# Softmax scale on ScalarE and the gate turned once per head pair, in an MLA and dilated-attention decoder trunk

## The chip, the cores and the metric

One core of one Trainium2 chip. The metric is the device time of one execution in microseconds (us); the kernel before was run three times.

## What is computed

The input is x, 256 tokens of width 2048, float32. Layer A is a multi-head latent attention layer of 16 heads, layer B a dilated sliding-window layer of 16 heads with three branches (dilations 1, 4, 16) that share one K/V. The change is in layer B. Cut to it:

```python
u = rms_norm(h, ln) @ w_in                     # queries of three branches, and a gate, per head
q = rms_norm(q_all[:, :, g], g_q[g])           # per branch g
s = where(valid, q @ k.T * E ** -0.5 + alibi, NEG_INF)
m = max(s); p = exp(s - m); den = sum(p)
o = p @ v / den                                # branches merged by their softmax denominators
return h + (o * silu(gate)) @ w_o
```

With 256 tokens the three branches are treated in one band of 384 scores for each head and each tile of 128 queries: 256 of branch 1 and 64 each of the residues of branches 4 and 16 on either half. One softmax over all of them gives the merged output.

## The kernel before

**Projections.** Every weight comes from HBM once, in steps of 128 x 1024 float32 (512 KB), through a ring of four slots (`RING`). SP issues the loads (L363). For each step ScalarE rounds the weights to float32r, the high part (`highs`, L478), VectorE subtracts to get the low part (`lows`, L794), and TensorE does three matmuls for each product (high by high, high by low, low by high; `three`, L1271): 12 matmuls of 512 columns per step. ScalarE may split a step once TensorE has used the slot three steps back (semaphore `slot_used`), VectorE follows ScalarE (`hi_ready`), and TensorE waits for VectorE (`lo_ready`).

**Layer B.** Its heads go in pairs, i = 0 to 7. A pair takes 40 steps, in 20 quarters s = 0 to 19 of two steps (`b_pair`, on every engine). Five accumulators follow each other: queries of branches 1 and 4 (Q01), keys of the same (K01), key of 16 and value of 1 (K2V0), values (V12), query of 16 and gate (Q2GATE). VectorE scales the rows by their reciprocal root mean square (`b_rows`, L864) and turns them in blocks of 32 (`b_blocks`, L1180), and ScalarE applies the gains (`gain_of`, L766). The gate's SiLU is computed by ScalarE and VectorE in `gate_tanhs` and `gates` at s = 19 and lies in `gate[:, 0]`, tokens on partitions.

**Attention** of pair i - 1 runs beside the projection of pair i, for i = 1 to 7, and the last beside the output projection (i = `PAIRS`), there at the steps `B_LAST_SLOTS` of one step each. A pair has four units u (two heads, two query tiles). `b_units(s)` gives the stages of a quarter: stage 0 of unit u is at s = u + 2, stage 1 one quarter later, and so on:

- stage 0: TensorE scores (`b_score`, L1514, L1519), VectorE adds the bias and takes the maximum (`band_mask`, L886, L891), ScalarE takes the exponential with its sum (`unit_exp`, L532)
- stage 1: VectorE takes the reciprocal of the sum (`unit_den`, L915) and multiplies the gate by it into `og` (`band_gate`, L899); both stand in `b_gates`, at the head of a quarter, in front of its first low part. TensorE turns three blocks of probabilities and `og` in one bank (`band_turn`, L1303), and ScalarE copies all 512 columns to `probT` (`unit_turned`, L516)
- stage 2: TensorE multiplies by the values (`band_pv`, L1536, L1540), VectorE multiplies by the turned gate (`band_out`, L904)
- stage 3: ScalarE and VectorE split the output in high and low (`band_store`, `band_low`).

In its order of work an engine does, in quarter s: TensorE the 24 projection matmuls and then its stages; ScalarE the first split, its stages (3, then 1, then 0), the second split; VectorE `b_gates`, the first low part, its stages 3, 2, 0, sums and blocks, the second low part. The query blocks of Q2GATE for the attention of pair i - 1 come at s = 0 and s = 1 of pair i, eight in each:

```python
if s < 2:
    for n in range(8 * s, 8 * s + 8):
        last = b_blocks(Q2GATE, 3, n)
    if s == 1:
        last.then_inc(blocked, 1)
```

`b_score` of unit 0 waits for ScalarE's gain of this query (`gained`), which waits for `blocked`. The order of every engine is written out by hand; all engines but TensorE run the middle pairs (2 to 7 in layer B, two per turn) in a hardware loop (`Fori`), TensorE has them written out.

## Time and profile before

| | |
|---|---|
| median of 3 runs | 1404.21 us (1403.74 to 1404.41) |
| the profiled execution's own time | 1404.01 us |
| its span | 1402.2 us |
| TensorE, VectorE, ScalarE, GpSimd busy | 99%, 75%, 50%, 7% of the span |
| TensorE's share of the chain that ended last | 94% |
| DMA | 252.49 MB, mean 180 GB/s |

The profile is of one execution. Its busy times are per engine; a TensorE matmul is pipelined, so its duration is longer than the distance to the next one, and start-to-start distances tell more. The time of the execution is its span and 1.8 us around it.

### The profile page before, as it was taken

The numbers are of one execution on the slowest core, as the hardware profiler recorded it, in microseconds if no ns is written. First come the engines' busy times: TensorE is split into PE (matmuls) and PEld (weight loads), VectorE is DVE, ScalarE is ACT, GpSimd is POOL, SyncE is SP. The second block draws the span as 40 slices with busy tenths as digits, with TensorE's granted clock in tenths as the row PEclk, the third lists the DMA queues.
The fourth block names the chain that finished last, engine by engine and source line by source line (L and its number), as shares of the span: only waits on it lengthen the run. The fifth ranks groups of instructions, "written<-read, shape, count | busy, mean of one in ns | idle before, by whom it ended". The sixth has DMA issues, their size and how long they took to land.

```text
span 1402.2 us, 20187 instructions
## 1 busy us (share of the span) xinstructions
PE 1395.2 (99%) x6648; PEld 1169.4 (83%) x6648; DVE 1046.5 (75%) x1969; ACT 706.6 (50%) x1032; POOL 102.5 (7%) x67
## 2 busy tenths in 40 slices
PE   9999999999999999999999999999999999999999
PEld 6888888888888888888888888888888888888887
DVE  6767767747667868877877877887887788789653
ACT  6555555646544544544544454544454445454442
POOL 0101001000010001000101100101010110010000
PEclk9999999999999999999999999999999999999999
DMA  9653544455556545645654654565556456555544
GB/s 355 232 173 125 166 143 142 147 190 179 183 187 203 191 151 180 205 155 180 182 194 149 197 181 163 183 198 167 166 188 189 159 186 194 160 181 190 171 165 150
DMA packets 71233, 252.49 MB, mean 180 GB/s; under 512 B 7904, under 2 KB 8288, under 8 KB 71136
## 3 DMA queue, kind: packets, MB, share of 16 engines
q1 hardware_dynamic: 70704, 249.95, 54.7%
q10 hardware_dynamic: 432, 1.31, 0.3%
q8 instruction: 53, 0.87, 0.2%
q14 instruction: 44, 0.36, 0.1%
HBM read 249.14 MB, written 2.10 MB: 179 GB/s over the span
## 4 chain that ended last, share of the span: by engine, by line
PE 94%; DVE 2%; issue 2%; ACT 1%; DMA 0%; POOL 0%; SPq 0%; DVEq 0%; POOLq 0%
PE acc L1271 85%; PE turn L1303 1%; PE score L1514 1%; PE pv_bank L1536 1%; PE score L1519 1%; PE pv_bank L1540 1%; DVE qT L1180 1%; PE pv_bank L1315 1%; PE score L1411 1%; PE score L1413 1%; DVE w_lo L794 1%; PE turn L1397 0%; DMA raw<-in_w_in 0%; PE og_bank L1323 0%; POOL rms L426 0%
## 5 line engine op out<-in xcount | busy, mean ns | idle before, releaser
L794 DVE TENSOR_TENSOR w_lo<-raw,w_hi 128x1024 fp32r<-128x1024 f32 x463 | 574.2, 1251 | 205.9 <-ACT w_hi L478 196.9
L478 ACT ACTIVATE w_hi<-raw 128x1024 fp32r<-128x1024 f32 x463 | 482.4, 1050 | 397.2 <-PE acc L1271 386.0
L1271 PE MATMUL acc<-w_hi,xa_hi 128*128 128x512 f32 x956 | 378.7, 396 | 0.6 <-DVE w_lo L794 0.4
L1271 PE MATMUL acc<-w_hi,xa_lo 128*128 128x512 f32 x956 | 372.8, 390 | 0.0
L1271 PE MATMUL acc<-w_lo,xa_hi 128*128 128x512 f32 x956 | 372.2, 389 | 0.0
L1271 PE MATMUL acc<-w_hi,xb_hi 128*128 128x512 f32 (+1 forms) x640 | 249.4, 390 | 0.0
L1271 PE MATMUL acc<-w_hi,xb_lo 128*128 128x512 f32 (+1 forms) x640 | 245.9, 384 | 0.0
L1271 PE MATMUL acc<-w_lo,xb_hi 128*128 128x512 f32 (+1 forms) x640 | 245.5, 384 | 0.0
L1271 PEld LDWEIGHTS acc<-w_hi,xa_lo 128*128 128x128 f32 x956 | 179.4, 188 | 37.9
L1271 PEld LDWEIGHTS acc<-w_hi,xa_hi 128*128 128x128 f32 x956 | 179.6, 188 | 37.5 <-issue 1.3
L1271 PEld LDWEIGHTS acc<-w_lo,xa_hi 128*128 128x128 f32 x956 | 179.7, 188 | 35.3
L426 POOL TENSOR_TENSOR rms<-ms,mhalf 128x4 f32<-128x4 f32 (+2 forms) x50 | 73.2, 1465 | 1050.6 <-DVE ms L850 855.4
L1271 PEld LDWEIGHTS acc<-w_hi,xb_lo 128*128 128x128 f32 x640 | 120.1, 188 | 22.7
L1271 PEld LDWEIGHTS acc<-w_lo,xb_hi 128*128 128x128 f32 x640 | 120.3, 188 | 22.1
L1271 PEld LDWEIGHTS acc<-w_hi,xb_hi 128*128 128x128 f32 x640 | 120.2, 188 | 22.0
L1180 DVE STREAM_TRANSPOSE kT<-rows 32x128 f32<-32x128 f32 x384 | 102.2, 288 | 4.5
L1271 PE MATMUL acc<-w_hi,oT_hi 128*128 128x512 f32 x256 | 102.3, 400 | 0.0
L1271 PE MATMUL acc<-w_hi,oT_lo 128*128 128x512 f32 x256 | 100.0, 391 | 0.0
L1271 PE MATMUL acc<-w_lo,oT_hi 128*128 128x512 f32 x256 | 99.7, 390 | 0.0
L1180 DVE STREAM_TRANSPOSE qT<-rows 32x256 f32<-32x256 f32 (+1 forms) x256 | 94.5, 369 | 4.1
L532 ACT ACTIVATE prob<-prob,top_neg 128x128 f32<-128x128 f32 (+1 forms) x64 | 34.3, 537 | 91.3 <-DVE top_neg L891 63.9
L516 ACT ACTIVATE probT<-turn 128x128 f32<-128x128 f32 (+1 forms) x64 | 29.7, 463 | 76.7 <-PE turn L1303 57.2
(178 smaller groups left out, 1061.4 us busy)
## 6 DMA issues: line engine op xcount, KB each, us to landing
raw<-in_w_b SPq DMA_DIRECT2D x320, 512.0 KB, 3.6
raw<-in_w_out_a SPq DMA_DIRECT2D x32, 512.0 KB, 3.3
raw<-in_w_out_b SPq DMA_DIRECT2D x32, 512.0 KB, 3.3
raw<-in_w_gate SPq DMA_DIRECT2D x30, 512.0 KB, 3.6
raw<-in_w_kv SPq DMA_DIRECT2D x16, 512.0 KB, 4.3
raw<-in_w_in SPq DMA_DIRECT2D x15, 512.0 KB, 6.2
raw<-in_w_q SPq DMA_DIRECT2D x16, 384.0 KB, 3.0
res<-in_x_tok SPq DMA_DIRECT2D x4, 512.0 KB, 7.8
```

What stands on the lines that cost most here:

```text
L426: nc.gpsimd.tensor_tensor(rms[:, 0:width], ms[:, 0:width], mhalf[:, 0:width], ALU.pow)\
L478: nc.scalar.activation(w[0][:, s, 0:width], raw[:, s, 0:width], ACT.Copy).then_inc(hi_ready, 1)
L516: last = nc.scalar.activation(dst, turn[:, 0:width], ACT.Copy)
L532: nc.scalar.activation(prob[:, u % 2, 0:width], prob[:, u % 2, 0:width], ACT.Exp, bias=top_neg[:, u:u + 1], accum_out=den[:, u:u + 1])\
L794: nc.vector.tensor_tensor(w[1][:, s, 0:width], raw[:, s, 0:width], w[0][:, s, 0:width].bitcast(F32), ALU.subtract).then_inc(lo_ready, 1)
L1180: last = nc.vector.transpose(dst, src)
L1271: last = nc.tensor.matmul(out, x(a), y(b), start=start and k == 0, stop=stop and k == 2, **more)
L1303: last = nc.tensor.transpose(turn[:, col:col + P], src, ident[:])
L1315: last = nc.tensor.matmul(pv, probT[:, k * P:(k + 1) * P], val, start=k == 0, stop=k == len(values) - 1)
L1411: nc.tensor.matmul(score[:, 0:n], qT[:, par * 512 + at:par * 512 + at + P], kT[:, k_0 + h * SEQ:k_0 + h * SEQ + n], start=True, stop=False)
L1413: nc.tensor.matmul(score[:, 0:n], q_ropes[par][:, at:at + P], kT[:, k_0 + 512:k_0 + 512 + n], start=False, stop=True).then_inc(scored, 1)
L1514: nc.tensor.matmul(score[:, P:P + SEQ], qT[:, h * SEQ + t * P:h * SEQ + (t + 1) * P], kT[:, h * SEQ:(h + 1) * SEQ], start=True, stop=True)
```

## The change

- `band_gate` is gone. In its place ScalarE multiplies the probabilities of a unit by the reciprocal sum in place, in stage 1, after a wait for `den_ready`, and TensorE's turn waits for that (`prob_scaled`). ScalarE's wait for `out_made` ahead of its copy is gone, and the copy has 384 columns.
- TensorE turns three blocks per unit instead of four. VectorE turns the gates of a pair, in 16 blocks of 32x128 from `gate[:, 0]` to `gate[:, 1]` (`gate_turn`): eight at s = 1 and eight at s = 2, there ahead of the mask of unit 0. `band_out` reads them there.
- All 16 query blocks of Q2GATE stand at s = 0.
- K01's blocks of both groups are one transpose of 32x256 each instead of two of 32x128.
- All `Fori` loops, on SP, GpSimd, ScalarE and VectorE, are Python loops: the instructions are written out. The diff shows two of them.

```diff
--- before.py
+++ after.py
@@ -216,6 +216,7 @@
         og_bank = ctx.enter_context(nc.psum_tensor("og_bank", [P, 512], F32))
         pv = pv_bank[:, 0:P]
         ogT = og_bank[:, 0:P]
+        gate_T = gate[:, 1].rearrange("p t d -> p (t d)")
         h_banks = (pv_bank, og_bank, score)
 
         def cst(name):
@@ -331,6 +332,8 @@
         den_ready = sem("den_ready")
         pv_ready = sem("pv_ready")
         og_ready = sem("og_ready")
+        prob_scaled = sem("prob_scaled")
+        gate_turned = sem("gate_turned")
         og_turned = sem("og_turned")
         o_ready = sem("o_ready")
         out_made = sem("out_made")
@@ -389,16 +392,16 @@
                     else:
                         load((i, MLA_STEPS), MLA_0 + s, w_gate[i, s - 2 if s < 4 else s - 4], STEP)
 
-            with sp.Fori(0, PAIRS - 1) as i:
+            for i in range(0, PAIRS - 1):
                 mla_pair(i, MLA_STEPS)
             mla_pair(PAIRS - 1, LAST_STEPS)
...
@@ -708,9 +711,10 @@
                     if stage == 3:
                         band_store((i - 1) * UNITS + u, i - 1, u)
                     if stage == 1:
-                        if u:
-                            act.wait_ge(out_made, (i - 1) * UNITS + u)
-                        unit_turned(b_round(i, u), u, BAND + P)
+                        act.wait_ge(den_ready, U + 1)
+                        at = prob[:, u % 2, 0:BAND]
+                        nc.scalar.activation(at, at, ACT.Copy, scale=den_inv[:, u:u + 1]).then_inc(prob_scaled, 1)
+                        unit_turned(b_round(i, u), u, BAND)
                     if stage == 0:
                         unit_exp(U, u, BAND)
 
@@ -891,17 +895,24 @@
                 nc.vector.tensor_scalar(top_neg[:, u:u + 1], top[:, u:u + 1], -1.0, None, ALU.mult)\
                     .then_inc(top_ready, 1)
 
-            def band_gate(U, u, g, gates_so_far):
+            def gate_turn(i, part):
+
+                if part == 0:
+                    dve.wait_ge(gate_done, i + GATE_FILLS)
+                for n in range(8 * part, 8 * part + 8):
+                    a, b = n // 4, n % 4
+                    src = gate[a * QUAD:(a + 1) * QUAD, 0].rearrange("p t (u d) -> p t u d", d=P)
+                    dst = gate_T[b * QUAD:(b + 1) * QUAD].rearrange("p (u t d) -> p t u d", t=TILES, d=P)
+                    last = nc.vector.transpose(dst[:, :, :, a * QUAD:(a + 1) * QUAD], src[:, :, :, b * QUAD:(b + 1) * QUAD])
+                if part == 1:
+                    last.then_inc(gate_turned, 1)
+
+            def band_out(U, i, u):
 
                 if u == 0:
-                    dve.wait_ge(gate_done, gates_so_far)
-                dve.wait_ge(den_ready, U + 1)
-                nc.vector.tensor_scalar(og[:, u % 2], g, den_inv[:, u:u + 1], None, ALU.mult).then_inc(og_ready, 1)
-
-            def band_out(U, u):
-
+                    dve.wait_ge(gate_turned, i)
                 dve.wait_ge(pv_ready, U + 1)
-                nc.vector.tensor_tensor(out[:, u % 2], pv, probT[:, BAND:BAND + P], ALU.mult).then_inc(out_made, 1)
+                nc.vector.tensor_tensor(out[:, u % 2], pv, gate_T[:, u * P:(u + 1) * P], ALU.mult).then_inc(out_made, 1)
 
             def band_low(U, i, u):
 
@@ -1163,38 +1174,39 @@
                     if stage == 1:
                         U = (i - 1) * UNITS + (B_UNIT_0 + u)
                         unit_den(U, u)
-                        band_gate(U, u, gate[:, 0, u % 2, (u // 2) * P:(u // 2 + 1) * P], i + GATE_FILLS)
 
             def b_blocks(f, k, n):
 
                 buf, x = (B_CHAIN_0 + k) % 2, qT if f in (Q01, Q2GATE) else kT
                 a, b = n // 4, n % 4
-                for first, groups, swap in {Q01: [(0, 2, 0)], K01: [(0, 1, 0), (1, 1, 1)], K2V0: [(0, 1, 1)],
-                                            Q2GATE: [(0, 1, 0)]}[f]:
-                    at = (first + 2 * (f in (K2V0, Q2GATE))) * 2 * SEQ
-                    col = QUAD * (a ^ 2 if swap else a)
-                    src = rows[a * QUAD:(a + 1) * QUAD, buf, :, first * 2 * P:(first + groups) * 2 * P]\
-                        .rearrange("p t (u d) -> p t u d", d=P)[:, :, :, b * QUAD:(b + 1) * QUAD]
-                    dst = x[b * QUAD:(b + 1) * QUAD, at:at + groups * 2 * SEQ]\
-                        .rearrange("p (u t d) -> p t u d", t=TILES, d=P)[:, :, :, col:col + QUAD]
-                    last = nc.vector.transpose(dst, src)
-                return last
+                groups = 2 if f in (Q01, K01) else 1
+                at, swapped = (0, 1) if groups == 2 else (2, 2)
+                if f in (Q01, Q2GATE):
+                    swapped = GROUPS
+                cols = [(at + g) * 2 * SEQ + QUAD * (a ^ 2 if at + g >= swapped else a) for g in range(groups)]
+                src = rows[a * QUAD:(a + 1) * QUAD, buf, :, 0:groups * 2 * P]\
+                    .rearrange("p t (g u d) -> p t g u d", u=2, d=P)[:, :, :, :, b * QUAD:(b + 1) * QUAD]
+                to = x[b * QUAD:(b + 1) * QUAD, cols[0]:cols[0] + QUAD]
+                parts = [list(d) for d in to.ap]
+                dst = bass.AP(to.tensor, to.offset, [parts[0], [P, TILES], [cols[-1] - cols[0] or QUAD, groups],
+                                                    [SEQ, 2], [1, QUAD]])
+                return nc.vector.transpose(dst, src)
 
             def b_attend(i, s, par_before):
                 if s == 0:
                     b_rows(i - 1, par_before, 3)
                     dve.wait_ge(rows_ready, i * 4 + B_CHAIN_0)
-                if s < 2:
-                    for n in range(8 * s, 8 * s + 8):
+                    for n in range(16):
                         last = b_blocks(Q2GATE, 3, n)
-                    if s == 1:
-                        last.then_inc(blocked, 1)
+                    last.then_inc(blocked, 1)
+                if s in (1, 2):
+                    gate_turn(i, s - 1)
                 for stage, u in b_units(s):
                     U = (i - 1) * UNITS + (B_UNIT_0 + u)
                     if stage == 3:
                         band_low(U, i - 1, u)
                     if stage == 2:
-                        band_out(U, u)
+                        band_out(U, i, u)
                     if stage == 0:
                         band_mask(U, (i - 1) * UNITS + u, u, alibi[:, u // 2, u % 2], i - 1)
 
@@ -1244,7 +1256,7 @@
 
             b_pair(0, 0, False)
             b_pair(1, 1, True)
-            with dve.Fori(0, (PAIRS - 2) // 2) as t:
+            for t in range(0, (PAIRS - 2) // 2):
                 b_pair(t * 2 + 2, 0, True)
                 b_pair(t * 2 + 3, 1, True)
             for k in range(OUT_STEPS):
@@ -1521,10 +1533,8 @@
 
             def band_turn(U, u, rnd):
 
-                pe.wait_ge(prob_ready, U + 1)
-                pe.wait_ge(og_ready, U + 1)
-                turn_rows(rnd, [(prob[:, u % 2, k * P:(k + 1) * P], k * P) for k in range(BAND // P)]
-                          + [(og[:, u % 2], BAND)])
+                pe.wait_ge(prob_scaled, U - B_UNIT_0 + 1)
+                turn_rows(rnd, [(prob[:, u % 2, k * P:(k + 1) * P], k * P) for k in range(BAND // P)])
 
             def band_pv(U, B, u, rnd):
```

How this moves the instructions, at three places. VectorE, from the gate's last operation at s = 19 to the first unit's reciprocal, beside pair 1 (`w_lo` is the low part of a step, `qT` the query blocks, `prob` the mask). Before:

```order
L935 TENSOR_SCALAR gate<-gate,r_half 128x256 x2
L794 TENSOR_TENSOR w_lo<-raw,w_hi 128x1024 x2
L864 TENSOR_TENSOR rows<-acc,rms 128x2x256
L1180 STREAM_TRANSPOSE qT<-rows 32x2x2x32 x8
L794 TENSOR_TENSOR w_lo<-raw,w_hi 128x1024 x2
L1180 STREAM_TRANSPOSE qT<-rows 32x2x2x32 x8
L794 TENSOR_TENSOR w_lo<-raw,w_hi 128x1024 x2
L886 ISA prob,top<-score,phase 64x384
```

After:

```order
L946 TENSOR_SCALAR gate<-gate,r_half 128x256 x2
L798 TENSOR_TENSOR w_lo<-raw,w_hi 128x1024 x2
L868 TENSOR_TENSOR rows<-acc,rms 128x2x256
L1193 STREAM_TRANSPOSE qT<-rows 32x2x2x32 x16
L798 TENSOR_TENSOR w_lo<-raw,w_hi 128x1024 x2
L906 STREAM_TRANSPOSE gate<-gate 32x2x2x32 x8
L798 TENSOR_TENSOR w_lo<-raw,w_hi 128x1024 x2
L906 STREAM_TRANSPOSE gate<-gate 32x2x2x32 x8
L890 ISA prob,top<-score,phase 64x384
```

The gate's 16 blocks stand between the rows and the first mask, as do all query blocks, before and now. ScalarE, beside pair 1, from the query's gain on (`w_hi` is the high part of a step, `rows<-acc` the squares). After:

```order
L770 ACTIVATE qT<-qT,gain 128x512
L535 ACTIVATE prob,den<-prob,top_neg 128x384
L481 ACTIVATE w_hi<-raw 128x1024 x2
L716 ACTIVATE prob<-prob,den_inv 128x384
L519 ACTIVATE probT<-turn 128x384
L535 ACTIVATE prob,den<-prob,top_neg 128x384
L512 ACTIVATE rows<-acc 128x1024
L481 ACTIVATE w_hi<-raw 128x1024 x2
L716 ACTIVATE prob<-prob,den_inv 128x384
```

The scale by the reciprocal sum (L716) is new; it stands behind the two splits and in front of the copy of the turned bank. VectorE in the last pair, now:

```order
L868 TENSOR_TENSOR rows<-acc,rms 128x2x256
L1193 STREAM_TRANSPOSE qT<-rows 32x2x2x32 x16
L798 TENSOR_TENSOR w_lo<-raw,w_hi 128x1024
L906 STREAM_TRANSPOSE gate<-gate 32x2x2x32 x8
L798 TENSOR_TENSOR w_lo<-raw,w_hi 128x1024 x2
L906 STREAM_TRANSPOSE gate<-gate 32x2x2x32 x8
L890 ISA prob,top<-score,phase 64x384
```

Before, eight query blocks, one low part, eight query blocks and two low parts stood between those rows and the mask.

## Rows read from the trace of the kernel before

**Rows 1.** Page, busy us (share of the span) and instructions.

```profile
PE 1395.2 (99%) x6648; PEld 1169.4 (83%) x6648; DVE 1046.5 (75%) x1969; ACT 706.6 (50%) x1032; POOL 102.5 (7%) x67
```

**Rows 2.** Groups by form: line, engine, op, names, shapes, xcount | busy us, mean ns | idle before.

```profile
L1180 DVE STREAM_TRANSPOSE kT<-rows 32x128 f32<-32x128 f32 x384 | 102.2, 288 | 4.5
...
L1180 DVE STREAM_TRANSPOSE qT<-rows 32x256 f32<-32x256 f32 x128 | 55.7, 435 | 2.1
...
L532 ACT ACTIVATE prob<-prob,top_neg 128x384 f32<-128x384 f32 x32 | 19.8, 617 | 63.9 <-DVE top_neg L891 63.9
...
L766 ACT ACTIVATE qT<-qT,gain 128x512 f32<-128x512 f32 x24 | 16.3, 709 | 4.0 <-DVE qT L1180 4.0
```

**Rows 3.** Timeline of PE, beside the projection of pair 2: start us, us, what, xcount.

```profile
609.89 0.60 PE L1514 MATMUL score<-kT,qT 128*128 128x256 f32 x2
610.32 0.61 PE L1519 MATMUL score<-kT,qT 128*128 128x128 f32 x4
610.68 0.48 PE L1271 MATMUL acc<-w_hi,xb_hi 128*128 128x512 f32 x1
...
616.23 0.49 PE L1303 MATMUL turn<-ident,prob 128*128 128x128 f32 x3
616.56 0.27 PE L1303 MATMUL turn<-ident,og 128*128 128x128 f32 x1
616.67 0.60 PE L1514 MATMUL score<-kT,qT 128*128 128x256 f32 x2
...
624.00 0.52 PE L1303 MATMUL turn<-ident,prob 128*128 128x128 f32 x3
```

**Rows 4.** Timeline of DVE, the same stretch; [idle us <-releaser].

```profile
594.39 0.69 DVE L845 TENSOR_REDUCE ss<-rows 128x4 f32<-128x512 f32 x1 [1.03 <-ACT rows L509]
...
599.55 2.51 DVE L1180 STREAM_TRANSPOSE qT<-rows 32x128 f32<-32x128 f32 x8
602.08 2.36 DVE L794 TENSOR_TENSOR w_lo<-raw,w_hi 128x1024 fp32r<-128x1024 f32 x2
...
607.03 1.23 DVE L794 TENSOR_TENSOR w_lo<-raw,w_hi 128x1024 fp32r<-128x1024 f32 x1
608.46 1.23 DVE L794 TENSOR_TENSOR w_lo<-raw,w_hi 128x1024 fp32r<-128x1024 f32 x1 [0.20 <-ACT w_hi L478]
611.16 0.55 DVE L886 CUSTOM_DVE_ANT_0 prob<-score,phase 64x384 f32<-64x384 f32 x1 [1.48 <-PE score L1519]
...
615.36 0.15 DVE L915 RECIPROCAL den_inv<-den 128x1 f32<-128x1 f32 x1
615.62 0.29 DVE L899 TENSOR_SCALAR og<-gate,den_inv 128x128 f32<-128x128 f32 x1
```

**Rows 5.** Timeline of ACT, behind unit 0's mask.

```profile
613.14 1.99 ACT L478 ACTIVATE w_hi<-raw 128x1024 fp32r<-128x1024 f32 x2
```

**Rows 6.** Timeline of DVE, unit 1 of the same pair.

```profile
623.61 0.29 DVE L899 TENSOR_SCALAR og<-gate,den_inv 128x128 f32<-128x128 f32 x1
```

**Rows 7.** Timeline of DVE and PE at the turn of the loop.

```profile
835.88 1.23 DVE L794 TENSOR_TENSOR w_lo<-raw,w_hi 128x1024 fp32r<-128x1024 f32 x1 [2.41 <-issue]
...
845.35 0.39 PE L1271 MATMUL acc<-w_hi,xb_lo 128*128 128x512 f32 x1
845.99 0.70 PE L1514 MATMUL score<-kT,qT 128*128 128x256 f32 x2 [0.25 <-ACT qT L766]
```

**Rows 8.** Timeline of DVE, last pair.

```profile
1306.59 2.51 DVE L1180 STREAM_TRANSPOSE qT<-rows 32x128 f32<-32x128 f32 x8
...
1315.21 0.54 DVE L886 CUSTOM_DVE_ANT_0 prob<-score,phase 64x384 f32<-64x384 f32 x1
```

**Rows 9.** Timeline of PE, last pair.

```profile
1313.71 0.70 PE L1514 MATMUL score<-kT,qT 128*128 128x256 f32 x2 [0.93 <-ACT qT L766]
...
1320.17 0.49 PE L1303 MATMUL turn<-ident,prob 128*128 128x128 f32 x3
```

**Rows 10.** Timeline of PE at the start; then windows: us, busy (x), PEclk, DMA.

```profile
1.85 4.99 PE L1340 MATMUL score<-probT 128*128 128x512 f32 x6 [1.85 <-POOL v L416]
...
1399.00:1402.20 3.20, 0.07 (x1) 0.00 (x0) 0.69 (x1) 0.00 (x0) 0.00 (x0) 1.00 0.44 164
1402.20:1404.00 1.80, 0.00 (x0) 0.00 (x0) 0.00 (x0) 0.00 (x0) 0.00 (x0) 0.51 0.00 0
```

More of the change, by code:

```diff
@@ L390, in mla_pair @@
                         load((i, MLA_STEPS), MLA_0 + s, w_gate[i, s - 2 if s < 4 else s - 4], STEP)
-            with sp.Fori(0, PAIRS - 1) as i:
+            for i in range(0, PAIRS - 1):
                 mla_pair(i, MLA_STEPS)
             mla_pair(PAIRS - 1, LAST_STEPS)
-            with sp.Fori(0, OUT_STEPS // 8) as j:
+            for j in range(0, OUT_STEPS // 8):
                 for q in range(8):
                     load((j, 8), OUT_A_0 + q, w_out_a[j, q], STEP)
-            with sp.Fori(0, PAIRS) as i:
+            for i in range(0, PAIRS):
                 for s in range(B_STEPS):
                     load((i, B_STEPS), B_0 + s, w_b[i, s], STEP)
-            with sp.Fori(0, OUT_STEPS // 8) as j:
+            for j in range(0, OUT_STEPS // 8):
                 for q in range(8):
@@ L432, in _ @@
             chain(1, TILES)
-            with pool.Fori(0, PAIRS) as i:
+            for i in range(0, PAIRS):
                 for s in range(MLA_STEPS):
@@ L459, in _ @@
             b_pair(0, False)
-            with pool.Fori(1, PAIRS) as i:
+            for i in range(1, PAIRS):
                 b_pair(i, True)
@@ L672, in _ @@
             mla_pair(1, 1, 1)
-            with act.Fori(0, (PAIRS - 4) // 2) as t:
+            for t in range(0, (PAIRS - 4) // 2):
                 mla_pair(t * 2 + 2, 0, 2)
@@ L777, in _ @@
             b_pair(1, 1, True)
-            with act.Fori(0, (PAIRS - 2) // 2) as t:
+            for t in range(0, (PAIRS - 2) // 2):
                 b_pair(t * 2 + 2, 0, True)
@@ L1126, in _ @@
             mla_pair(1, 1, 1, 0)
-            with dve.Fori(0, (PAIRS - 4) // 2) as t:
+            for t in range(0, (PAIRS - 4) // 2):
                 mla_pair(t * 2 + 2, 0, 2, t + 1)
@@ L1246, in _ @@
             b_pair(1, 1, True)
-            with dve.Fori(0, (PAIRS - 2) // 2) as t:
+            for t in range(0, (PAIRS - 2) // 2):
                 b_pair(t * 2 + 2, 0, True)
```

## The prediction

> **What bounds the kernel now.** I read the page's busy times first: TensorE (PE) is busy for 99% of the span [rows 1]. So the time is the sum of TensorE's own work and its waits, and an edit counts only through these two. Then I read the first units beside the projection of pair 2 of layer B in the timeline, one engine at a time. On TensorE two score groups and one turn group show the rhythm of a unit: score, 24 projection matmuls, turn, score [rows 3]. On VectorE the reader is to see which stretches have no idle time in front, and where it does wait [rows 4]. ScalarE's row there gives the two operations that sit between the exponential and the next split [rows 5].
>
> The link that matters is the one behind the first mask of a pair. The mask of unit 0 starts at 611.16, the reciprocal of the denominator ends at 615.51, the scaled gate at 615.91, and TensorE turns at 616.23 [rows 3, 4]. Between mask and reciprocal lie the exponential, two splits on ScalarE, of which VectorE's next low part needs the first, and that low part itself [rows 4, 5]: 4.35 us from mask to reciprocal. So before the change the turn has 0.3 us to spare, and VectorE as a whole has 0.20 us and 1.48 us of idle time ahead of the mask, 1.68 us together [rows 4]. That is the whole reserve of this stretch. It can't be enlarged by work saved earlier in the pair, since VectorE waits at 594.39 for the squares that end the projection of the pair before [rows 4], and everything from there to 608.26 runs without a gap.
>
> **The change, part by part.**
>
> (a) *TensorE's turn of the gate goes.* One 128x128 turn takes 0.11 us from start to start (616.56 to 616.67) [rows 3]. 32 units: -3.5 us, all of it on the path.
>
> (b) *VectorE turns the gates, in 16 pieces of 32x128 per pair.* The nearest row is the query blocks of the same shape: 8 in 2.51 us, 0.314 each [rows 4]. Per pair 5.03 us. Eight come in step 1 and eight in step 2, both ahead of the first mask; the 16 query blocks, now all in step 0, were ahead of it before too. So 5.03 us of new work meets 1.68 us of reserve, and the mask starts 3.35 us later, at 614.5.
>
> (c) *ScalarE scales the probabilities, VectorE no longer scales the gate.* The scale is 128x384 in SBUF. The nearest rows are the exponential on the same tile, 617 ns, and the 128x512 gain in place, 709 ns [rows 2]; I take 0.60. It replaces 0.29 on VectorE [rows 4] in the same place of the chain. For unit 0: 615.51 + 3.35 + 0.05 to hand over + 0.60 + 0.10 = 619.6, where TensorE was ready at 616.23: **3.4 us of new wait per pair**. Seven pairs run this way beside projections: +23.7.
>
> (d) *Unit 1.* Its turn already waited: the scaled gate ends at 623.90, the turn starts at 624.00 [rows 3, 6]. The chain is the same, with 0.60 in the place of 0.29 and a shorter turn of unit 0, whose gain stands in (a): +0.33, seven times +2.3. Units 2 and 3 have 0.8 us more room, since no squares of a chain lie in their link: 0.
>
> (e) *The written-out loops.* At the loop's turn VectorE stood 2.41 us for issue, and the first score of that pair started 0.64 us after the last projection matmul, where such matmuls begin 0.23 apart (24 of them from 610.68 to 616.23), and then took 0.1 us longer [rows 3, 7]: 0.5 us, at two turns of this loop, -1.0. Elsewhere the loops' register instructions cost nothing that I find: from mask to turn it is 5.07 us in a loop pair and 4.96 in the last pair, which was never in a loop [rows 3, 4, 8, 9], and that 0.1 is TensorE's, not the chain's.
>
> (f) *The last pair* runs beside the output projection, in steps half as long. VectorE has no gap from 1306.59 to the mask at 1315.21 [rows 8]. Now 16 query blocks (5.03), one low part (1.23), 8 gate pieces (2.52), two low parts (2.36) and 8 gate pieces (2.52) come first: mask at 1320.3. The turn follows 4.35 + 0.75 = 5.1 us later, at 1325.4, against 1320.17 [rows 9]: +5.3. The query blocks are ready earlier, so the 1.1 us that TensorE lost ahead of its score at 1313.71 goes, but that is inside the 5.3, as it only lengthens the later wait.
>
> (g) *Both K groups in one transpose.* 128 of 32x256 at 435 ns take the place of 256 at 288 [rows 2]: VectorE saves 18 us over the kernel, in steps 10 to 17. It lies ahead of the wait at 594.39, so nothing of it reaches TensorE: 0. ScalarE's copy of the turned bank is 128 columns shorter and no longer waits for VectorE's output product; the exponential behind it waits for the mask anyway: 0.
>
> Sum: -3.5 + 23.7 + 2.3 - 1.0 + 5.3 = **+26.8**, on the profiled execution's 1404.0: 1430.8.
>
> (h) *TensorE's clock.* In the trace it is granted in full (2.4 GHz) as long as TensorE works; 3.1 us after the last matmul it falls to the lower level, 1.2 GHz [rows 10]. At the start, six 128x512 float32 matmuls took 4.99 us, about 0.8 us from start to start, where 256 columns take 0.22 [rows 3, 10]: the lower level, for some 4.5 us, which costs 2.2 us. In the last pair TensorE will be ready at about 1319.5 (its score 1.1 us earlier than before, a low part behind the gate pieces 0.4 us later) and stand until 1325.4, for 5.9 us, so I count one fall there; the seven waits of 3.4 us are barely longer than the 3.1 us in the row, and I count one or two falls among them at a little under 2.2 each. That makes +3.7 and the forecast **1434.5**. The profiled execution lies 0.2 us below the median of 1404.21, which changes nothing.
>
> A rule of the Trainium skill, "TensorE: Matmul & The Clock Gate", section on HAM oscillation, says that a TensorE that idles between groups of matmuls is throttled to half and starts the next group cold, each time. By that rule the sum would be that of rival 1. "VectorE: DVE Perf Modes", rules for kernel authors, speaks against the change: a 128x128 transpose belongs on TensorE if PSUM will do. Here 32 turns of 0.11 us on TensorE become 128 pieces of 0.314 on VectorE, and the trace bears the rule out as far as VectorE's reserve is gone; with a reserve of 5 us the rule would be wrong here by the 3.5 us of (a).
>
> **Rivals.**
>
> 1. *Every wait lets the clock fall.* Then eight falls of 2.2: 1430.8 + 17.6 = 1448.4. For it: the fall at 3.1 us. Against it: seven waits are hardly longer, and the few small matmuls around them are work too. Chance 0.13.
>
> 2. *The waits are smaller than I think.* The gate pieces run as fast as the K blocks, whose mean is 288 ns where the query blocks begin 314 ns apart [rows 2, 4], so at 0.28 at best, and the scale takes 0.45. That is 0.5 and 0.15 less per pair, 5.2 in eight, and the clock doesn't fall: 1430.8 - 5.2 = 1425.6. For it: the shapes are alike. Against it: the gate's pieces are written with the query blocks' pattern. Chance 0.12.
>
> 3. *VectorE's reserve covers the gate pieces (the other side).* If VectorE's order left the first mask at its old place, only (a), (d), (e) and the vanished 1.1 us would be left: 1404.0 - 3.5 + 2.3 - 1.0 - 1.1 = 1400.7, or 0.24% faster. It decides at 1.7 to 2.0 us of work ahead of the mask: the pieces would have to take 0.12 us each, or most of them to run behind the mask. The order of the program and the row at 2.51 us speak against it. Chance 0.06.
>
> 4. *The program doesn't do what it says.* VectorE's longer stream of written-out instructions could also stall for fetching, as at the loop's turn, or the five-dimensional transposes of K could run piece by piece and be no faster than two; both make VectorE later, but before the wait at 594.39 there is slack. Within 5 us of the forecast, either way. Chance 0.05, inside the range.
>
> **Numbers.** Forecast 0.64, the rivals 0.13, 0.12, 0.06, 0.05. The range reaches down past rival 2, by the 0.4 us that each of eight waits may be off, and up to rival 1: 1422 to 1448. A difference of 0.2% (2.8 us) is about what can be told from none. Slower by more than that: all but rival 3 and what lies between it and rival 2, 0.91; within it 0.03; faster 0.06, rival 3.
>
> **What would show it.** In the profile of the changed kernel, TensorE's turn of unit 0 should wait for ScalarE's scaling by about 3.4 us in seven pairs and by about 6 in the last; between the query blocks and the first mask VectorE should have no idle time; the turn of unit 1 should wait some 0.5 us; the score's wait for the query gain should be gone. The granted clock should show a dip near 1325. I am wrong if the first mask starts less than 1 us behind its score, if the gate pieces take under 0.2 us, or if TensorE's waits are at a projection, for a low part, and not at the turn.

## The result, and the profile after

The changed kernel takes 1437.44 us, the median of four runs (1435.33 to 1438.38), where the kernel before takes 1404.2. The ratio is 1.0236, with a 95% interval of 1.0224 to 1.0248: 2.4% slower, 3 us above the forecast. The profiled execution took 1438.38 us, with a span of 1436.4 us against 1402.2 before: 34.2 us to account for.

The page of the kernel after, busy us by engine and then the chain that ended last:

```profile
PE 1403.3 (98%) x6616; PEld 1173.8 (82%) x6616; DVE 1065.1 (74%) x1937; ACT 723.2 (50%) x1064; POOL 101.5 (7%) x67
...
PE 84%; DVE 13%; ACT 2%; issue 1%; DMA 0%; POOL 0%; SPq 0%; ACTq 0%; DVEq 0%
```

TensorE has 32 matmuls fewer than before [rows 1] and is busy for longer: part of its work ran at a lower clock, as the windows below show. Its share of the chain fell from 94% to 84%, and VectorE stands in the chain with 13%. The page's 40 slices are no help here; the waits are only a few microseconds each.

The groups by form (line, engine, operation, names, shapes, count, busy us, mean ns, idle before) that answer to [rows 2], and the new ones:

```profile
L1193 DVE STREAM_TRANSPOSE kT<-rows 32x256 f32<-32x256 f32 x128 | 55.8, 436 | 2.6
...
L906 DVE STREAM_TRANSPOSE gate<-gate 32x128 f32<-32x128 f32 x128 | 38.7, 303 | 1.8
...
L716 ACT ACTIVATE prob<-prob,den_inv 128x384 f32<-128x384 f32 x32 | 19.7, 616 | 11.3 <-DVE den_inv L926 11.3
...
L1315 PE MATMUL turn<-ident,prob 128*128 128x128 f32 x144 | 27.6, 284 | 27.4 <-ACT prob L716 27.4
```

The last row names the loss: TensorE stood 27.4 us in front of its turns, waiting for ScalarE's scaled probabilities. The gate pieces and the scale cost what they were taken for, 303 and 616 ns.

Where that wait comes from stands in the timeline beside the projection of pair 2, the stretch of [rows 3]. TensorE (start us, us, what, count, idle before and its releaser), and then score, last matmul and turn of unit 0 in the last pair:

```profile
614.86 0.60 PE L1526 MATMUL score<-kT,qT 128*128 128x256 f32 x2
...
620.97 0.39 PE L1283 MATMUL acc<-w_hi,xb_lo 128*128 128x512 f32 x1
624.39 0.55 PE L1315 MATMUL turn<-ident,prob 128*128 128x128 f32 x3 [3.03 <-ACT prob L716]
...
632.36 0.55 PE L1315 MATMUL turn<-ident,prob 128*128 128x128 f32 x3 [0.21 <-ACT prob L716]
...
1340.00 0.59 PE L1526 MATMUL score<-kT,qT 128*128 128x256 f32 x2
...
1346.61 0.39 PE L1283 MATMUL acc<-w_hi,oT_lo 128*128 128x512 f32 x1
1352.70 0.90 PE L1315 MATMUL turn<-ident,prob 128*128 128x128 f32 x3 [5.70 <-ACT prob L716]
```

Matmuls of 512 columns begin 0.23 us apart, so TensorE was ready at 621.20 and stood 3.19 us; in the last pair it was ready at 1346.84 and stood 5.86. (The brackets say a little less, because the end of a matmul is modelled. Starts are what I count with.)

VectorE in the same stretch, the rows that answer to [rows 4], with ScalarE's scale behind the reciprocal, and then the last pair's mask:

```profile
599.36 0.69 DVE L849 TENSOR_REDUCE ss<-rows 128x4 f32<-128x512 f32 x1 [1.03 <-ACT rows L512]
...
604.52 5.05 DVE L1193 STREAM_TRANSPOSE qT<-rows 32x128 f32<-32x128 f32 x16
609.60 2.36 DVE L798 TENSOR_TENSOR w_lo<-raw,w_hi 128x1024 fp32r<-128x1024 f32 x2
611.88 2.50 DVE L906 STREAM_TRANSPOSE gate<-gate 32x128 f32<-32x128 f32 x8
614.39 2.36 DVE L798 TENSOR_TENSOR w_lo<-raw,w_hi 128x1024 fp32r<-128x1024 f32 x2
616.78 2.52 DVE L906 STREAM_TRANSPOSE gate<-gate 32x128 f32<-32x128 f32 x8
619.34 0.55 DVE L890 CUSTOM_DVE_ANT_0 prob<-score,phase 64x384 f32<-64x384 f32 x1
...
623.53 0.16 DVE L926 RECIPROCAL den_inv<-den 128x1 f32<-128x1 f32 x1
623.72 0.61 ACT L716 ACTIVATE prob<-prob,den_inv 128x384 f32<-128x384 f32 x1 [0.42 <-DVE den_inv L926]
...
1347.65 0.55 DVE L890 CUSTOM_DVE_ANT_0 prob<-score,phase 64x384 f32<-64x384 f32 x1
```

Behind the read of the squares at 599.36 there is no bracket on any row up to the mask: VectorE never waits. The two idle pieces of [rows 4], 0.20 and 1.48 us, are gone, and the mask comes 19.98 us after that read where it came 16.77 after it before. It starts 4.5 us behind the start of its score. From there the chain is as long as it was: mask to turn 5.05 us (5.07 before), because the 0.6 of the scale replaced the 0.29 of the gate's product and the 0.3 us that the turn had to spare.

The second loss stands in the granted clock. Windows of 12 us around four of the first-unit waits (window, length, busy us and counts of PE, PEld, DVE, ACT, POOL, then PEclk, DMA share, GB/s):

```profile
497.00:509.00 12.00, 8.95 (x31) 7.13 (x30) 6.10 (x14) 7.20 (x11) 0.69 (x1) 0.72 0.30 90
620.00:632.00 12.00, 8.97 (x48) 7.36 (x46) 7.28 (x16) 7.54 (x12) 1.48 (x1) 1.00 0.30 97
742.00:754.00 12.00, 8.95 (x38) 7.25 (x37) 7.05 (x13) 7.52 (x12) 1.89 (x1) 0.86 0.27 87
...
1346.00:1358.00 12.00, 6.30 (x23) 5.06 (x22) 6.53 (x19) 4.84 (x9) 0.00 (x0) 0.72 0.47 146
```

Of the seven waits beside projections, all of 3.19 to 3.21 us, three more have 0.86 and one more has 1.00: the clock fell at five of seven and in the last pair. What a fall does to the work shows in TensorE's rows behind the first of these waits:

```profile
497.56 0.39 PE L1283 MATMUL acc<-w_hi,xb_lo 128*128 128x512 f32 x1
501.00 0.90 PE L1315 MATMUL turn<-ident,prob 128*128 128x128 f32 x3 [3.05 <-ACT prob L716]
...
505.54 0.63 PE L1283 MATMUL acc<-w_hi,xa_lo 128*128 128x512 f32 x1
505.96 0.63 PE L1283 MATMUL acc<-w_hi,xa_hi 128*128 128x512 f32 x1
...
507.41 0.39 PE L1283 MATMUL acc<-w_lo,xa_hi 128*128 128x512 f32 x1
507.64 0.40 PE L1283 MATMUL acc<-w_hi,xa_lo 128*128 128x512 f32 x1
...
511.45 0.50 PE L1315 MATMUL turn<-ident,prob 128*128 128x128 f32 x3
```

At the lower level (1.2 GHz) matmuls begin 0.42 us apart, then 0.23 again. From the turn of unit 0 to that of unit 1 it takes 10.45 us here and 7.97 in pair 2 (624.39 to 632.36), where the clock did not fall.

### The profile page after: what moved, and what is told of

Same layout as the page of the kernel before. It is cut to its first block, busy times and chain, and to the rows that moved or that the text cites. A ratio compares the mean times of both kernels' runs of the same rounds, so it can differ in the third digit from the quotient of the medians.

```text
span 1436.4 us, 17781 instructions
## 1 busy us (share of the span) xinstructions
PE 1403.3 (98%) x6616; PEld 1173.8 (82%) x6616; DVE 1065.1 (74%) x1937; ACT 723.2 (50%) x1064; POOL 101.5 (7%) x67
## 4 chain that ended last, share of the span: by engine, by line
PE 84%; DVE 13%; ACT 2%; issue 1%; DMA 0%; POOL 0%; SPq 0%; ACTq 0%; DVEq 0%
PE acc L1283 75%; DVE w_lo L798 5%; DVE qT L1193 3%; DVE gate L906 3%; PE turn L1315 1%; PE pv_bank L1546 1%; PE score L1531 1%; PE pv_bank L1550 1%; PE score L1526 1%; DVE prob L890 1%; PE pv_bank L1327 1%; PE score L1423 1%; PE score L1425 1%; DVE ss L849 1%; ACT rows L512 1%
## 5 line engine op out<-in xcount | busy, mean ns | idle before, releaser
L1193 DVE STREAM_TRANSPOSE kT<-rows 32x256 f32<-32x256 f32 (+1 forms) x256 | 94.5, 369 | 4.5
L512 ACT ACTIVATE rows<-acc 128x512 f32<-128x512 f32 (+2 forms) x50 | 39.0, 780 | 38.8 <-PE acc L1283 38.8
```

The costliest lines, as they stand in the source:

```text
L512: nc.scalar.activation(rows[:, buf, :, 0:width], acc[:, pair, :, 0:width], ACT.Square)\
L1193: return nc.vector.transpose(dst, src)
```

## The experiments

Two theories were to be told apart. **Order**: the time comes from the gate pieces standing ahead of the first mask, with VectorE's reserve exceeded, and the clock adds to it. **Parts**: the new operations cost it, the scale on ScalarE above all, or the written-out loops. Each kernel below was timed against the kernel before on its own chip (medians 1403.82 to 1404.01).

### Leaving the gate's transposes out: e1_no_gate_turn

```diff
-                if u == 0:
-                    dve.wait_ge(gate_turned, i)
...
-                if s in (1, 2):
-                    gate_turn(i, s - 1)
```

> The change without VectorE's turn of the gates (its 16 transposes per pair and the wait for them are left out, so layer B's output is multiplied by what lies in the second half of the gate tile instead of the gate). Theory: the 5.03 us of transposes ahead of the first mask are the cause of the waits of 3.2 us (seven) and 5.9 us (one) and, through them, of the clock's falls. Then all of these go: unit 0's turn waits at most 0.3 us, and the time is 1404.2 - 3.5 (TensorE's turns) - 1.0 (loops) - 1.1 (score of the last pair) + 1.5 (unit 1) = about 1400. Rival: ScalarE's scale in the link, or all 16 query blocks in one quarter, is what makes unit 0 late: then waits of 1 us or more stay at unit 0 and the time stays above 1410.

Measured: 1402.28 us, ratio 0.9988 (0.9979 to 0.9997). The waits of its TensorE (line, releaser, total us, times, longest):

```profile
PE turn L1311 <- ACT prob L716: 2.9, 8, 1.0
```

The whole rest of the change, scale included, is a gain of 1.7 us. All seven waits of unit 0 beside projections are gone, the clock never fell, and what is left is 0.4 us at unit 1 (0.7 in one pair) and 1.2 at unit 0 of the last pair. That last wait was not expected. It is the 1.1 us of the score's wait, moved to the turn: in that pair VectorE had no gap before the change either [rows 8], and from the last turn of the pair before to this one it takes 90.40 us, against 90.56 before the change. So the transposes on VectorE carry 35.2 us, though VectorE is idle for a quarter of the span.

### The loops alone: e2_loops_only

```diff
-            with dve.Fori(0, (PAIRS - 2) // 2) as t:
+            for t in range(0, (PAIRS - 2) // 2):
```

The same edit at every `Fori` of the kernel before.

> The kernel before with all hardware loops written out and nothing else. Theory: only the stall of the score at two turns of layer B's loop goes, 0.5 us each: 1403.2, that is 1.0 us faster. Rival: the register instructions on VectorE and ScalarE or the loops of layer A cost more than I find: 1400 or less. Second rival: the longer program costs fetching: 1405 or more.

Measured: 1402.63 us, ratio 0.9990 (0.9981 to 0.9999), 1.4 us less; the forecast had 1.0. The two late scores behind the loop's turn are gone; the score of the last pair still waits:

```profile
PE score L1514 <- ACT qT L766: 0.9, 1, 0.9
```

### The same waits with TensorE kept at work: e3_busy_wait

```diff
+                if u == 0:
+                    for _ in range(24 if rnd == b_round(PAIRS, 0) else 12):
+                        nc.tensor.matmul(og_bank[:], xa[0][:, 0, 0:P], ..., start=True, stop=True)
                 pe.wait_ge(prob_scaled, U - B_UNIT_0 + 1)
```

> The change with TensorE kept at work during its wait for unit 0: 12 matmuls of 512 columns into a bank that nothing reads, ahead of the wait (24 in the last pair), 2.7 us of the 3.2 and 5.4 of the 5.9. Theory: the clock no longer falls, and the 11.5 us that its low stretches cost in the trace go, the waits stay: about 1426, granted clock 1.00 throughout. Rival: the low stretches cost nothing of their own, since VectorE's chain would hold TensorE anyway: 1437 or more.

Measured: 1429.94 us, ratio 1.0183 (1.0168 to 1.0199). Its TensorE at the same place:

```profile
619.65 2.88 PE L1538 MATMUL og_bank<-xa_hi 128*128 128x512 f32 x12
622.86 0.55 PE L1315 MATMUL turn<-ident,prob 128*128 128x128 f32 x3 [0.33 <-ACT prob L716]
```

The turn comes no earlier: 3.21 us behind the moment TensorE was ready, against 3.19. But the granted clock is 1.00 throughout. With the waits' length kept, the falls are worth 1437.44 - 1429.94 = 7.5 us by the medians, 8.2 by the two spans. The spans also differ by something that isn't the clock: this trace has a wait in its very first steps that the changed kernel's hasn't.

```profile
13.41 0.48 PE L1283 MATMUL acc<-w_hi,xa_hi 128*128 128x512 f32 x1 [0.58 <-DVE w_lo L798]
```

Behind it TensorE runs 0.9 us later, and its first turn still does (501.87 against 501.00); the kernel before has such a wait too, of 0.41 us, at 13.04. Without it the falls are worth 9.1 by the spans. I had expected 1426, taking the whole loss in the slow stretches for the price. It isn't: behind a fall the second turn has no wait left (511.45 above stands without a bracket), while here it waits 0.4 us in every pair. A fall costs 9.2 - 8.0 = 1.2 us in four pairs (745.37 to 754.58 is 9.21), 2.5 in the first, where the slow stretch is twice as long, and 2.0 in the last.

### Six of sixteen pieces moved behind the second mask: e4_moved

```diff
-                if s in (1, 2):
-                    gate_turn(i, s - 1)
+                if s == 1 and i < PAIRS:
+                    gate_turn(i, 0, 5)
+                if s == 4 and i == PAIRS:
+                    gate_turn(i, 10, 16)
...
+                        if u < 2:
+                            gate_turn(i, *(((0, 5), (5, 10)) if i == PAIRS else ((5, 10), (10, 16)))[u])
```

`gate_turn` takes first and last piece here. Five pieces stand ahead of the first mask, five behind it, six behind the second.

> The change with the 16 gate transposes of a pair in other places: 5 ahead of the first mask (1.57 us, inside the reserve of 1.68), 5 behind the first mask and 6 behind the second, where VectorE waits for ScalarE's exponential and split anyway; in the last pair 5, 5 and 6 behind the masks of units 0 and 1 and ahead of unit 0's output. Theory: it is only where the transposes stand that costs; the mask starts as before, unit 0's turn waits 0.3 to 0.5 us, no fall of the clock: 1401 to 1404, at or below the time of before. Rival: VectorE's work as such is too much in these quarters, and the transposes behind the masks make units 1 or 2 late instead: 1410 or more.

Measured: 1403.85 us, ratio 0.9999 (0.9990 to 1.0008). VectorE's first mask, and TensorE's two turns, beside pair 2:

```profile
607.15 1.55 DVE L906 STREAM_TRANSPOSE gate<-gate 32x128 f32<-32x128 f32 x5
608.72 2.36 DVE L798 TENSOR_TENSOR w_lo<-raw,w_hi 128x1024 fp32r<-128x1024 f32 x2
611.40 0.55 DVE L890 CUSTOM_DVE_ANT_0 prob<-score,phase 64x384 f32<-64x384 f32 x1 [0.32 <-PE score L1535]
...
616.48 0.53 PE L1319 MATMUL turn<-ident,prob 128*128 128x128 f32 x3
...
624.69 0.55 PE L1319 MATMUL turn<-ident,prob 128*128 128x128 f32 x3 [0.49 <-ACT prob L716]
```

Every instruction of the change is still there, and 33.6 us are gone. The mask waits for its score again. Five pieces take 1.55 us and 0.32 are left, so the reserve is 1.87 us, a little more than the 1.68 that the brackets of [rows 4] add up to. **Order** it is. Unit 1 pays a little, 0.67 us a pair (8.21 from turn to turn, where e5_early_den below has 7.54 without a wait), since six pieces now stand ahead of its reciprocal.

### The reciprocal right behind the mask: e5_early_den

```diff
                         if u < 2:
                             gate_turn(...)
+                        unit_den(U, u)
...
-                    if attend:
-                        b_gates(i, s)
                     lows((i, B_STEPS), B_0 + 4 + 2 * s)
```

On top of e4_moved, and the same in the last pair.

> As the run with the moved gate transposes (1403.85), and the reciprocal of a unit's sum stands right behind its mask on VectorE instead of behind the low part that follows. Theory: what is left as waits there, 0.65 us at unit 1 in seven pairs and 1.2 us at unit 0 of the last, comes from the reciprocal's place behind the squares' sums and the low part; ScalarE's scale then follows its second split at once, 5.5 us behind the mask at unit 1 where TensorE comes 5.9 behind it. The seven waits go (-4.6) and 0.4 of the last: 1399 us, 0.35% faster than before. Rival: ScalarE itself is late, or VectorE's wait for the exponential now holds up the sums and low parts: 1402 or more.

Measured: 1398.37 us against 1403.83, ratio **0.9960 (0.9947 to 0.9974)**: 0.4% faster than the kernel before, a small gain but clear of the noise. Unit 1's reciprocal (VectorE), its scale (ScalarE) and the turns (TensorE):

```profile
618.69 1.90 DVE L906 STREAM_TRANSPOSE gate<-gate 32x128 f32<-32x128 f32 x6
620.62 0.16 DVE L926 RECIPROCAL den_inv<-den 128x1 f32<-128x1 f32 x1
...
622.12 0.60 ACT L716 ACTIVATE prob<-prob,den_inv 128x384 f32<-128x384 f32 x1
...
615.78 0.49 PE L1309 MATMUL turn<-ident,prob 128*128 128x128 f32 x3
...
623.31 0.50 PE L1309 MATMUL turn<-ident,prob 128*128 128x128 f32 x3
```

In e4_moved this reciprocal ran at 623.84, behind a low part; here it is done before ScalarE's split ends, the scale follows without a bracket, and both turns stand directly behind their matmuls. One wait is left in layer B, 0.64 us in the last pair.

### The early reciprocal without the swap: e8_early_gate

On e2_loops_only, `unit_den` and `band_gate` moved behind `band_mask` in the same way, and nothing else of the change.

> The kernel before with its loops written out (1402.63) and the reciprocal and the scaled gate right behind the mask, TensorE's turn of the gate kept. It tells what of a gain of the early reciprocal needs the change at all. Theory: unit 1's wait of 0.12 us in seven pairs goes, nothing else: 1401.8; the 3.5 us of TensorE's 32 turns are then the difference to the version with the early reciprocal on the changed kernel, less the last pair's wait. Rival: the early reciprocal alone does as much, 1399 or less, and the change brings nothing.

Measured: 1401.5 us, ratio 0.9984 (0.9975 to 0.9993). This is 2.3 us less than the kernel before. So of e5's 5.5 us, 1.4 are the loops, 1.0 the earlier reciprocal (turn to turn 7.62 us in place of 7.74), and 3.1 the rest of the change. That rest is the swap for the most part: a pair lasts 117.31 us in e5_early_den and 117.70 here, 0.39 for four turns that were priced at 0.11 each. It also has the moved query blocks, the K transposes and the last pair's waits (0.64 us at the turn there, 1.1 at the score here), which no run takes apart.

### The scale's price: e7_scale_twice

```diff
-                        ... scale=den_inv[:, u:u + 1]).then_inc(prob_scaled, 1)
+                        ... scale=den_inv[:, u:u + 1]).then_inc(scaled_once, 1)
+                        act.wait_ge(scaled_once, (i - 1) * UNITS + u + 1)
+                        nc.scalar.activation(at, at, ACT.Copy, scale=1.0).then_inc(prob_scaled, 1)
```

On e4_moved: a second pass over the probabilities.

> As the run with the moved gate transposes (1403.85), and ScalarE passes over the probabilities a second time with factor 1.0, 0.6 us more in the link from reciprocal to turn. Theory: the scale stands wholly in the link: unit 1's wait grows from 0.65 to 1.3, unit 0's from 0 to about 0.4 and the last pair's by 0.65: 7 x 1.05 + 0.65 = 8.0, 1411.9. Rival: ScalarE has time there and the scale is hidden: 1405 or less.

Measured: 1411.97 us, ratio 1.0058 (1.0043 to 1.0073), 8.1 us above e4_moved.

```profile
PE turn L1322 <- ACT prob L719: 11.5, 15, 1.6
```

All of the second pass lands on the path of units 0 and 1, none of it on units 2 and 3: 0.53 at unit 0 and 0.59 at unit 1 in seven pairs, 0.56 in the last, 8.4 in all. The scale is on the path; it is cheap because 0.6 replaced 0.29 and 0.3 of slack.

### The query blocks back in two eights: e6_blocks_8_8

```diff
-                    for n in range(16):
-                        last = b_blocks(Q2GATE, 3, n)
-                    last.then_inc(blocked, 1)
+                if s < 2:
+                    for n in range(8 * s, 8 * s + 8):
+                        last = b_blocks(Q2GATE, 3, n)
+                    if s == 1:
+                        last.then_inc(blocked, 1)
```

> The change with the query blocks at their old places, eight in each of the first two quarters. Theory: what counts is the sum of VectorE's work ahead of the first mask, which stays: 1436 to 1438, the seven waits still 3.2 us. Rival: all 16 in one quarter hold up the low parts and so the splits: 1434 or less.

Measured: 1439.21 us, ratio 1.0250 (1.0234 to 1.0266), 1.8 above the changed kernel and 1.2 above the range expected. The seven waits are 3.32 us, the clock fell at six of them, and the last pair's score waits again:

```profile
1342.54 0.70 PE L1528 MATMUL score<-kT,qT 128*128 128x256 f32 x2 [0.93 <-ACT qT L770]
```

So that move of the change takes away the score's wait, which lies inside the later one, as (f) said: the turn waits 5.28 us here and 5.86 there, and from the last turn of the pair before to this one it takes 95.73 and 95.59 us. It takes 0.1 us off each of the seven. Two medians of four runs, 1.8 us apart with a different number of falls, say little beyond that.

### Twelve and fourteen pieces ahead: e9_ahead_12, e10_ahead_14

```diff
-                    gate_turn(i, s - 1)
+                    gate_turn(i, *((0, 8), (8, 12))[s - 1])
...
+                        if u == 0:
+                            gate_turn(i, 12, 16)
```

With 14 in place of 12 in the second. They set the length of the wait, to see how the clock's falls go with it.

> The change with 12 of the 16 gate transposes ahead of the first mask and 4 behind it. It asks whether the falls of the clock hang on the length of the wait. Theory: the waits shrink by 4 x 0.314 = 1.25 us, from 3.2 to 1.9 in seven pairs and from 5.9 to 4.6 in the last; the clock no longer falls in the seven, where it fell five times of seven at 3.2, and may fall once in the last. With 10.0 less of waits and some 5 less of low clock: 1421 to 1424. Rival: the falls hang on the number of waits and not on their length; they stay, and the time is 1427 or more.

> The change with 14 of the 16 gate transposes ahead of the first mask and 2 behind it. Theory: waits of 2.6 us in seven pairs and 5.2 in the last, 5.0 less in sum; the clock falls at fewer of the seven than at 3.2 us, none to two of them: 1425 to 1431. Rival: as often as at 3.2 us: 1432 or more.

Measured: 1422.31 us, ratio 1.0132 (1.0115 to 1.0149), and 1429.77 us, ratio 1.0186 (1.0169 to 1.0203). The seven waits are 1.9 and 2.5 us. A piece moved ahead makes the wait 0.31 us longer. Windows of e9_ahead_12 around the second wait and of the last pair:

```profile
616.00:628.00 12.00, 10.02 (x53) 8.17 (x52) 8.53 (x18) 7.84 (x12) 2.05 (x1) 1.00 0.38 118
...
1330.00:1342.00 12.00, 7.59 (x31) 6.07 (x30) 7.56 (x20) 5.86 (x10) 0.00 (x0) 0.86 0.48 162
```

e10_ahead_14, the second and third waits, in windows and in TensorE's timeline:

```profile
617.50:629.50 12.00, 9.61 (x50) 7.84 (x49) 7.88 (x20) 7.26 (x12) 1.20 (x1) 1.00 0.39 124
739.00:751.00 12.00, 9.62 (x40) 7.66 (x39) 7.79 (x15) 7.74 (x12) 2.23 (x1) 0.86 0.33 96
...
622.17 0.55 PE L1317 MATMUL turn<-ident,prob 128*128 128x128 f32 x3 [2.39 <-ACT prob L716]
742.48 0.55 PE L1317 MATMUL turn<-ident,prob 128*128 128x128 f32 x3 [2.38 <-ACT prob L716]
```

The two waits are the same to 0.01 us, and the clock fell at one of them; in all it fell at three of the seven, where at most two were expected. Over the four kernels, with the falls of the profiled execution of each and the mean granted clock of all four runs of each:

| wait of unit 0 | kernel | clock fell | mean clock, four runs |
|---|---|---|---|
| 1.9 us | e9_ahead_12 | 0 of 7 | 0.998 to 0.999 |
| 2.5 us | e10_ahead_14 | 3 of 7 | 0.994 to 0.995 |
| 3.2 us | the change | 5 of 7 | 0.990 to 0.994 |
| 3.3 us | e6_blocks_8_8 | 6 of 7 | 0.990 to 0.992 |
| 4.6 to 5.9 us, last pair | all four | 4 of 4 | |

Five of seven against six of seven says nothing by itself; none at 1.9 us against some at 2.5 and most above 3 is what the mean clocks bear out.

## Why the prediction was right, and where it was off

**The mechanism** was the one forecast: 5 us of pieces against 1.68 us of reserve ahead of a mask whose chain had no slack. e4_moved shows it by moving nothing but those pieces. Rival 3, the other side, is what e4_moved became: the reserve does hold five pieces, but the program put sixteen there. Its -1.1 for the score's wait would not have come, though, since that wait only moves to the turn (e1_no_gate_turn). Rival 2 is out: a piece and the scale took what their nearest rows said.

Term by term, measured in the traces:

- (a) -3.5 forecast: 0.39 a pair, -3.1 found.
- (b), (c) +23.7 forecast, seven waits of 3.20 = 22.4 found. The mask came 3.21 us later, not 3.35: the pieces took 5.02 us, as priced, but the reserve was 1.8 to 1.9 us and not 1.68, as e4_moved shows too. The scale's 0.60 held, and so did its chain.
- (d) +2.3 forecast: where the clock didn't fall, turn to turn is 7.97 against 7.77 before (616.23 to 624.00 [rows 3]), and the 0.1 that stands in (a) comes on top: 0.3 a pair, 2.1.
- (e) -1.0 forecast, -1.4 found.
- (f) +5.3 forecast: 5.86 of wait, less the 1.08 of the score that is gone, plus 0.5 for the low part behind the gate pieces (from the score at 1340.00 it takes 6.84 until TensorE is ready at 1346.84; in pair 2 it takes 6.34): 5.3. The wait itself was forecast at 5.9. (The prediction's own figures, 1325.4 less 1320.17, make 5.2.)
- (g) 0: the K transposes took 128 x 436 ns, as taken, and no row of TensorE got earlier for it. In e1_no_gate_turn the terms (a), (d) and (e) make -2.4 us, and -1.7 was measured, so no gain is left there for it or for the shorter copy.
- Sum without the clock: 25.3 found, 26.8 forecast. e3_busy_wait, with the waits and without the falls, is 25.9 above its kernel before.

**(h) is the term that failed in size.** I counted one fall in the last pair and one or two among the seven, at 2.2 us each or a little less, and put down +3.7, which is less than even two falls at 2.2 (4.4). There were six falls in the profiled execution: 4 x 1.2 + 2.5 + 2.0 = 9.3 us, and 25.3 + 9.3 = 34.6 against the 34.2 of the spans. By the medians the term is 7.5, twice what I gave it.

Two errors of opposite sign met. The falls were too few, since I took the one fall in the trace, 3.1 us behind a last matmul [rows 10], for what every fall would need, and the seven waits for barely long enough; e10_ahead_14 has falls at 2.5 us. And the price was too high for most: from turn to turn a fall takes 9.2 us where 7.5 is the time without any wait, so it costs 1.6 to 1.7 in itself, and 0.4 of that is taken back, since unit 1's wait is gone. Six falls at 2.2 would have made 13.2. The price had no sure source either. It came from six slow matmuls at the start, which I put down to the lower level by their durations alone: the granted clock in the same trace reads 1.00 from 0 to 6.2 us, and the two readings don't agree. The terms before (h) were 0.9 to 1.5 us too high in sum (25.9 by e3_busy_wait, 25.3 by the traces), which hid a part of its error, so that the forecast lies nearer to the time than its account of the clock deserves.

Rival 1, a fall at every wait, stayed a rival: five of seven is near it, but its 2.2 us for each is not; two more falls of 1.2 would put it 2.4 us above the profiled execution, at 1440.8, not at 1448. The Trainium skill, "TensorE: Matmul & The Clock Gate", section on HAM oscillation, has a TensorE that waits long enough between groups of matmuls start the next one cold each time. The counts agree for the waits of 4.6 us and more, four of four. For the shorter ones they don't bear out "each time": none of seven at 1.9 us, three of seven at 2.5, five of seven at 3.2.

The Trainium skill, "VectorE: DVE Perf Modes", rules for kernel authors, gives the 128x128 transpose to TensorE if its result may go to PSUM. This case agrees as long as the pieces stand ahead of the mask, and does not in e5_early_den, where VectorE does them in its idle time and the kernel is 3.1 us faster than e8_early_gate, which leaves them on TensorE.

The signs given beforehand: the turn of unit 0 waited in seven pairs and the last, VectorE had no idle time ahead of the mask, the score's wait was gone, the dip in the clock was there. Unit 1's wait was 0.4 where I wrote 0.5, and appeared only where the clock had not fallen; and there were six dips, where I had named a place only for the one at the end.

Still open: why the clock falls at one wait of 2.5 us and not at the next of the same length. The work around them is the same, and no run varied when the wait comes while keeping its length.

## What to carry to other kernels

An engine that is idle for a quarter of the span may still have only 1.7 us of room where work is added: count its idle time between its last fixed point and the instruction that another engine waits for, and put added work behind that instruction, not ahead of it. The same 16 transposes cost 35.2 us with all of them ahead of the mask and 1.6 with eleven behind it (1437.44 and 1403.85 against the 1402.28 of e1_no_gate_turn). Where a change makes TensorE wait anew, look for a lost clock besides: here it came at some of the waits of 2.5 to 3.3 us and at all of the four above 4.5, and cost 1.2 to 2.5 us each time.

## What was not expected of the hardware

- A fall need not show in the operation right behind the wait. TensorE of the changed kernel behind the third of the seven waits:

```profile
745.37 0.55 PE L1315 MATMUL turn<-ident,prob 128*128 128x128 f32 x3 [3.05 <-ACT prob L716]
...
746.35 1.06 PE L1531 MATMUL score<-kT,qT 128*128 128x128 f32 x4
...
754.58 0.50 PE L1315 MATMUL turn<-ident,prob 128*128 128x128 f32 x3
```

  The turn takes its 0.55 us as at full clock, the score behind it 1.06 us where 0.61 is usual: the clock went to the lower level with TensorE at work again (granted clock 1.00 from 745.0 to 745.9 us, 0.50 from 746.0 to 747.0).

- Equal waits do not fare equally, and the same kernel differs from run to run: the four runs of the change have a mean granted clock of 0.990 to 0.994, the longest (1438.38 us) the lowest and the shortest (1435.33) the highest. That spread of 3 us is wider than that of e3_busy_wait, whose four runs, at a clock of 1.00, lie within 0.6.
- A fall is partly taken back: the engines that feed TensorE run on while it is slow, so the next small wait vanishes (unit 1's 0.4 us, gone behind each of the five falls beside projections).
